# Latent queries prepared in the retention stage, and unsplit fp32 products at the start of two stages

## The reference, cut to what matters

```
cq, ckv, kr, rq, rk, rv, rg, ga, gb = split(x @ w_in)
q     = (rms_norm(cq, q_norm_g) @ w_q_up)           # latent queries, 256 wide
o_ret = retention_chunked(rope(rq), rope(rk) * RET_DK ** -0.5, rv)   # 4 heads
o_mla = attention(q, rms_norm(ckv), rope(kr), ...)  # 8 heads
mixed = (sigmoid(ga) * (o_mla @ w_mla_o) + sigmoid(gb) * (ret @ w_ret_o)) @ w_out
h     = layer_norm(ALPHA * x + mixed)
out   = layer_norm(ALPHA * h + shared_expert(h) + routed_experts(h))
```

## Time and profile before

| what | value |
|---|---|
| median of three runs | 1898.04 us |
| the three runs | 1894.51, 1898.04, 1899.26 us |
| the profiled execution | 1883.99 us |
| its span, first to last instruction | 1882.2 us |
| mean granted TensorE clock | 0.979 of 2.4 GHz |
| start of attention, mixing, trunk in the span | 497.2, 729.0, 827.9 us |
| MB moved, packets | 411.62, 133020 |

### The profile page before, as it was taken

The page is one execution under the profiler, slowest core; times in us unless marked ns, Lnnn a source line. Parts: engine busy times, 40 slices in busy tenths (PEclk is TensorE's granted clock), DMA queues, the critical chain, the costliest instruction groups (busy, mean ns, idle before and its releaser), DMA issues. The chain is left out here.

```text
span 1882.2 us, 24592 instructions
## 1 busy us (share of the span) xinstructions
PE 1780.7 (95%) x8660; PEld 1222.0 (65%) x8660; DVE 690.2 (37%) x1482; ACT 422.0 (22%) x862; POOL 351.7 (19%) x288
## 2 busy tenths in 40 slices
PE   7999999999899998999999999999999999999990
PEld 7999999999655556988865444444444444544440
DVE  3112444443256555645775222222222222222225
ACT  3111221322345453211100011111111111111114
POOL 0000330430100000001156111222222222222213
PEclk9999999999899999999999999999999999999995
DMA  6331633442312217441252689999999999999966
GB/s 213 100 103 52 189 108 107 154 129 72 127 31 71 61 42 269 169 155 59 82 227 47 259 313 379 380 386 381 388 369 365 370 368 370 369 368 367 349 183 215
DMA packets 133020, 411.62 MB, mean 219 GB/s; under 512 B 17620, under 2 KB 79092, under 8 KB 115332
## 3 DMA queue, kind: packets, MB, share of 16 engines
q1 hardware_dynamic: 108418, 319.77, 45.5%
q0 software_dynamic: 21504, 73.87, 15.0%
q10 hardware_dynamic: 3026, 17.04, 2.2%
HBM read 339.11 MB, written 73.96 MB: 219 GB/s over the span
## 5 line engine op out<-in xcount | busy, mean ns | idle before, releaser
L2397 PE MATMUL e_G<-wb,pages 128*128 128x512 f32 x1072 | 471.1, 592 | 1.8 <-DMA wb<-in_w_exp_gu 1.5
L2397 PEld LDWEIGHTS e_G<-wb,pages 128*128 128x128 f32 x1072 | 203.5, 190 | 258.3 <-issue 258.3
L2388 PE MATMUL e_Y<-mixT,e_aT 128*128 128x512 f32 x544 | 246.0, 595 | 2.4 <-ACT e_aT L2259 2.4
L2230 POOL DMA_INDIRECT d_base<-e_y_sb,e_s_idx x68 | 107.7, 1584 | 584.9 <-DMA d_base<-e_y_sb,e_s_idx 531.0
L2388 PEld LDWEIGHTS e_Y<-mixT,e_aT 128*128 128x128 f32 x544 | 98.0, 190 | 101.2 <-issue 100.6
L1293 PE MATMUL gate_ps<-x_hi,gw_hi 128*128 128x352 f32 x464 | 151.7, 327 | 1.4 <-DVE r_srg L1096 1.4
L181 PE MATMUL ps<-w_hi,x_hi 128*128 128x244 f32 x512 | 142.9, 279 | 9.8 <-DVE x_lo L235 8.7
L1293 PE MATMUL gate_ps<-x_hi,gw_lo 128*128 128x352 f32 x464 | 149.4, 322 | 0.0
L1293 PE MATMUL gate_ps<-x_lo,gw_hi 128*128 128x352 f32 x464 | 149.0, 321 | 0.0
L181 PE MATMUL ps<-w_hi,x_lo 128*128 128x244 f32 x512 | 142.1, 278 | 0.0
L181 PE MATMUL ps<-w_lo,x_hi 128*128 128x244 f32 x512 | 141.7, 277 | 0.0
(11 more groups left out here) (410 smaller groups left out, 2708.0 us busy)
## 6 DMA issues: line engine op xcount, KB each, us to landing
wb<-in_w_exp_gu SPq DMA_DIRECT2D x64, 2048.0 KB, 13.0
mixT<-in_w_exp_dn SPq DMA_DIRECT2D x68, 1024.0 KB, 7.3
gw_sb<-in_w_gate SPq DMA_DIRECT2D x20, 512.0 KB, 6.8
d_proj<-o_sb SPq DMA_DIRECT2D x8, 1098.0 KB, 6.2
d_gateT<-r_g_out ACTq DMA_DIRECT2D x16, 528.0 KB, 2.7
pages<-in_cache_both SPq DMA_DIRECT2D x64, 128.0 KB, 2.0
wb<-in_w_exp_gu ACTq DMA_DIRECT2D x4, 2048.0 KB, 15.2
w_sb<-in_w_in SPq DMA_DIRECT2D x7, 976.0 KB, 11.1
```

Of the source, the lines that this page charges most:

```text
L2230: g.indirect_dma_start(base, bass.IndirectOffsetOnAxis(ap=s_idx[s][:, 0:1], axis=0), y_sb[:, c, :], None, compute_op=ALU.add).then_inc(y_o ...
L2388: mm = t_.matmul(Y[q][:], aT[:, c, k, :], w_d[:, s, k, q * 512:(q + 1) * 512], start=k == 0, stop=k == 1)
L2397: mm = t_.matmul(G[c], xT[:, c, k, :], w_gu[s][:, :, k, :], start=k == 0, stop=k == KD - 1)
```

## The change

Latent queries: their load moves from the start of attention to SP's list in retention's last head, into the memory of `raw_q` and `raw_k` (now one tile) once both rotations are done. VectorE squares them, sums them and takes the mean after `nbias` of the last head; GpSimd takes the power; VectorE scales them after `gained`. ScalarE's squares, VectorE's and GpSimd's steps and SP's wait leave attention. The tile `cq` in attention is placed at the same address.

Mixing: A of j = 0 is made from the unsplit fp32 tiles (12 products of 352 columns, c outermost, 24 matmul records), so its weights are not split, and oT is split after rT and the first half of j = 1's weights. VectorE's `unit` is cut in two, and the first two A multiplications of j = 0 are put between the last oT splits. SP's load of j = 2's weights goes ahead of the two 2 MB loads.

Trunk: the first four of eight k steps of `out(0, 1)` are made from unsplit fp32 tiles ahead of everything else (4 products of 512 columns, 8 records); the right half of w_out is split from k = 4 on; the order becomes out_raw, out(0, 0), out(0, 1) without those steps, out(1, 0), out(1, 1).

```diff
@@ attention: tiles and loads @@
-        stat = sb("stat", [P, 2, NT])
-        mhalf = sb("mhalf", [P, NT])
...
-        cq = turned_flat[:, 0:NT * QL].rearrange("p (t c) -> p t c", t=NT)
+        cq = nc.alloc_sbuf_tensor_at("t_cq", [P, NT, QL], F32, offset=cq_at)
         rt = turned_flat[:, NT * (QL + KVL):NT * (QL + KVL) + 4 * TC].rearrange("p (a s c) -> p a s c", a=2, s=2)
-        sq_q = turned_flat[:, 5120:5120 + QL]
...
             sp.dma_start(wuv[:], a["w_uv"]).then_inc(w_kv_in, 16)
-            sp.dma_start(cq, pv[:, :, 0:QL]).then_inc(cq_in, 16)
             sp.dma_start(qg[:], a["q_norm_gT"]).then_inc(const_in, 16)
-            sp.wait_ge(cq_in, 16)
             sp.dma_start(w_q.rearrange("p k b n -> p (k b n)"), a["w_q_ext"]).then_inc(w_in_s, 16)
...
-            g.memset(mhalf[:], -0.5).then_inc(pl, 1)
             g.memset(bd[:], 0.0).then_inc(bd_clear, 1)
-            pool.wait_ge(pl, 1)
-            pool.wait_ge(dv, 1)
-            g.tensor_tensor(stat[:, 1, :], stat[:, 0, :], mhalf[:], ALU.pow).then_inc(pl, 1)
-
-            pool.wait_ge(pl, 2)
+            pool.wait_ge(bd_clear, 1)
             pool.wait_ge(krT_ok, 2)
...
-                if u == 4:
-                    dve.wait_ge(sq_ok, NT)
-                    v.tensor_scalar(stat[:, 0, :], stat[:, 0, :], 1.0 / QL, RMS_EPS, ALU.mult, ALU.add).then_inc(dv, 1)
-            dve.wait_ge(pl, 2)
-            v.tensor_tensor(cq, cq, stat[:, 1, :].unsqueeze(2).broadcast_to([P, NT, QL]), ALU.mult).then_inc(cq_ok, 1)
...
-            act.wait_ge(cq_in, 16)
-            for t in range(NT):
-                act.wait_ge(sq_ok, t)
-                s_.activation(sq_q, cq[:, t, :], ACT.Square, accum_out=stat[:, 0, t:t + 1]).then_inc(sq_ok, 1)
...
-            pe.wait_ge(cq_ok, 1)
@@ retention @@
+        cq_at = nc.sbuf_base
+        raw_qk = sb("raw_qk", [P, 2, NT, P])
+        raw_q, raw_k = raw_qk[:, 0], raw_qk[:, 1]
+        cq = raw_qk[:].rearrange("p a t c -> p (a t c)").rearrange("p (t c) -> p t c", t=NT)
...
-        tq = sb("tq", [P, 2, NT, 64])
-        tk = sb("tk", [P, 2, NT, 64])
+        tqk = sb("tqk", [P, 2, 2, NT, 64])
+        tq, tk = tqk[:, 0], tqk[:, 1]
+        cq_squares = tqk[:].rearrange("p a b t c -> p (a b t c)").rearrange("p (t c) -> p t c", t=NT)
+        cq_s = sb("cq_s", [P, 2, NT])
...
+                    if i == 3 and h == HR - 1:
+                        sp.wait_ge(q_rot, 6 * HR)
+                        sp.wait_ge(k_rot, 6 * HR)
+                        sp.dma_start(cq, pv[:, :, 0:QL]).then_inc(cq_in, 16)
...
+            pool.wait_ge(cq_var, 1)
+            g.tensor_tensor(cq_s[:, 1, :], cq_s[:, 0, :], mhalf[:], ALU.pow).then_inc(cq_rstd, 1)
...
+            dve.wait_ge(cq_in, 16)
+            dve.wait_ge(q_rot, 6 * HR)
+            dve.wait_ge(k_rot, 6 * HR)
+            v.tensor_tensor(cq_squares, cq, cq, ALU.mult).then_inc(cq_dv, 1)
+            dve.wait_ge(cq_dv, 1)
+            v.tensor_reduce(cq_s[:, 0, :], cq_squares, AX.X, ALU.add).then_inc(cq_dv, 1)
+            dve.wait_ge(cq_dv, 2)
+            v.tensor_scalar(cq_s[:, 0, :], cq_s[:, 0, :], 1.0 / QL, RMS_EPS, ALU.mult, ALU.add).then_inc(cq_var, 1)
             gained(HR - 1)
+            dve.wait_ge(cq_rstd, 1)
+            v.tensor_tensor(cq, cq, cq_s[:, 1, :].unsqueeze(2).broadcast_to([P, NT, QL]), ALU.mult).then_inc(cq_dv, 1)
+            dve.wait_ge(cq_dv, 3)
@@ mixing @@
+            def weights(j):
+                sp.wait_ge(w_hi_ok, 2 * j - 3)
+                sp.wait_ge(w_lo_ok, 2 * j - 3)
+                sp.dma_start(w_raw[:, j % 2], a["w_mix"][j]).then_inc(w_in_s[j % 2], 16)
+            sp.wait_ge(a_done, 3)
+            weights(2)
             sp.wait_ge(o_hi_ok, 4)
             sp.wait_ge(o_lo_ok, 4)
             sp.dma_start(wo_raw, a["w_out"].rearrange("(k p) n -> p k n", p=P)[:, :, 0:512]).then_inc(wo_in, 16)
@@ -1427,9 +1435,8 @@
             sp.wait_ge(r_lo_ok, 4)
             sp.dma_start(pages[:, 0:KD * 512].rearrange("p (k n) -> p k n", k=KD), a["w_out"].rearrange("(k p) n -> p k n", p=P)[:, :, 512:D]).then_inc(wo1_in, 16)
             for j in range(2, KD):
-                sp.wait_ge(w_hi_ok, 2 * j - 2)
-                sp.wait_ge(w_lo_ok, 2 * j - 2)
-                sp.dma_start(w_raw[:, j % 2], a["w_mix"][j]).then_inc(w_in_s[j % 2], 16)
+                if j > 2:
+                    weights(j)
 
...
-            weights(0, 0)
-            for k in range(4):
-                s_.copy(oT_hi[:, k], oT[:, k]).then_inc(o_hi_ok, 1)
             weights(0, 1)
             act.wait_ge(r_in, 64)
             for k in range(4):
                 s_.copy(rT_hi[:, k], r_raw[:, k]).then_inc(r_hi_ok, 1)
-            for q in range(2):
-                weights(1, q)
+            weights(1, 0)
+            for k in range(4):
+                s_.copy(oT_hi[:, k], oT[:, k]).then_inc(o_hi_ok, 1)
+            weights(1, 1)
             for q in range(2):
                 weights(2, q)
...
-                dve.wait_ge(w_hi_ok, 2 * j + q + 1)
+                dve.wait_ge(w_hi_ok, 2 * j + q)
...
-            weights(0, 0)
-            for k in range(4):
+            def o_part(k):
                 dve.wait_ge(o_hi_ok, k + 1)
                 v.tensor_tensor(oT_lo[:, k], oT[:, k], oT_hi[:, k].bitcast(F32), ALU.subtract).then_inc(o_lo_ok, 1)
             weights(0, 1)
             for k in range(4):
                 r_part(k)
-            for q in range(2):
-                weights(1, q)
+            weights(1, 0)
+            for k in range(3):
+                o_part(k)
+            first_product(0, 0)
+            o_part(3)
+            first_product(0, 1)
+            weights(1, 1)
             for j in range(KD):
                 for c in range(3):
                     if j == 3:
                         wo_residue(3 * c, min(3 * c + 3, KD))
                     if j == 4 and c == 0:
                         dve.wait_ge(wo_lo_ok, KD)
-                    unit(j, c)
+                    if j or c == 2:
+                        first_product(j, c)
+                    second_product(j, c)
                     if c == 0 and j and j + 1 < KD:
                         for q in range(2):
                             weights(j + 1, q)
@@ -1536,7 +1552,9 @@
...
-                    pe.wait_ge(w_lo_ok, 2 * j + 1)
+                    pe.wait_ge(w_lo_ok, 2 * j)
+                if u == 3:
+                    pe.wait_ge(o_lo_ok, 4)
...
-                    pe.wait_ge(w_lo_ok, 2 * j + 2)
+                    pe.wait_ge(w_lo_ok, 2 * j + 1)
                 if u >= 3:
                     pe.wait_ge(tb_ok, u - 2)
                 part(B[u % 3], 4, rT_hi, rT_lo, j, c).then_inc(b_done, 1)
-            def first_part(out, w0, hi, lo, hi_ok, lo_ok, done):
-
-                pe.wait_ge(w_lo_ok, w0 // 4 + 1)
+            pe.wait_ge(w_in_s[0], 16)
+            for c in range(3):
                 for k in range(4):
-                    pe.wait_ge(hi_ok, k + 1)
-                    pe.wait_ge(lo_ok, k + 1)
-                    for c in range(3):
-                        at = slice(c * TC, (c + 1) * TC)
-                        for s, (w, x) in enumerate(((w_hi, hi), (w_hi, lo), (w_lo, hi))):
-                            mm = t_.matmul(out[c][:, 0:TC], w[:, 0, w0 + k, :], x[:, k, at], start=k == 0 and s == 0, stop=k == 3 and s == 2)
-                        if k == 3:
-                            mm.then_inc(done, 1)
-            first_part(A, 0, oT_hi, oT_lo, o_hi_ok, o_lo_ok, a_done)
-            first_part(B, 4, rT_hi, rT_lo, r_hi_ok, r_lo_ok, b_done)
+                    mm = t_.matmul(A[c][:, 0:TC], w_raw[:, 0, k, :], oT[:, k, c * TC:(c + 1) * TC], start=k == 0, stop=k == 3)
+                mm.then_inc(a_done, 1)
+            pe.wait_ge(w_lo_ok, 1)
+            for k in range(4):
+                pe.wait_ge(r_lo_ok, k + 1)
+                for c in range(3):
+                    at = slice(c * TC, (c + 1) * TC)
+                    for s, (w, x) in enumerate(((w_hi, rT_hi), (w_hi, rT_lo), (w_lo, rT_hi))):
+                        mm = t_.matmul(B[c][:, 0:TC], w[:, 0, 4 + k, :], x[:, k, at], start=k == 0 and s == 0, stop=k == 3 and s == 2)
+                    if k == 3:
+                        mm.then_inc(b_done, 1)
             for j in range(1, KD):
                 for c in range(3):
@@ trunk @@
             sp.wait_ge(wo1_hi_ok, KD)
             sp.wait_ge(wo1_lo_ok, KD)
+            sp.wait_ge(y_raw, 1)
             sp.dma_start(w_gu[:, :, 0:256], a["w_sh_gate"].rearrange("(k p) n -> p k n", p=P)).then_inc(w_in_s, 16)
...
-            for k in range(KD):
+            for n in range(KD):
+                k = (n + 4) % KD
                 s_.copy(wo1_hi[:, k], w_gu[:, k]).then_inc(wo1_hi_ok, 1)
...
-                dve.wait_ge(wo1_hi_ok, k + 1)
+            for n in range(KD):
+                k = (n + 4) % KD
+                dve.wait_ge(wo1_hi_ok, n + 1)
                 v.tensor_tensor(wo1_lo[:, k], w_gu[:, k], wo1_hi[:, k].bitcast(F32), ALU.subtract).then_inc(wo1_lo_ok, 1)
```

(38 more changed lines are left out.)

6 lines of the change are left out of this document (2 added, 4 removed).

## The result

| | before | changed |
|---|---|---|
| median of 5 runs | 1898.04 us | 1887.49 us |
| lowest and highest | 1894.51, 1903.57 us | 1883.25, 1891.36 us |
| profiled execution | 1883.99 us, span 1882.2 | 1884.30 us, span 1882.5 |

The ratio is 0.9937, with a 95% interval of 0.9915 to 0.9958: 10.55 us less by the medians, 8 to 16 by the interval. The two profiled executions, though, are equally long. Each stage on which the change works is shorter in the new profile, and what was won is gone again at trunk's end. Both have to be explained.

A forecast was written before the change was run, and what follows sets the result against it. TensorE, busy 95% of the span, was taken as the bound. Attention 6.6, mixing 3.7 - 1.4 and trunk 4.1 - 1.4 sum to 11.6 us, so 1898.04 becomes 1886.4 us, range 1881 to 1894.

The forecast's parts named there:

- I take 6.6, because the idle time that preceded the fall is gone: Attention's start: 3.55 us idle before the value product and 3.03 us of its lower clock level both won.
- the zero: Retention's last head: the latent queries' load and arithmetic, moved there, are covered by TensorE's last gate unit and cost 0.
- clock term: Mixing's start: a short clock fall after about 2 us idle takes 1.4 us off the 3.7 us gain.
- the 4.1 of the text: Trunk's start: end at 850.4 against 854.58, 4.1 us won at the full clock.
- the 1.9 us row: Wait at trunk's end, followed by a 0.57 clock over 3.2 us; taken as model for a 1.4 us loss.
- The 1.4 us at both starts: Mixing and trunk: a short clock fall after about 2 us idle, costing 1.4 us each.
- carrying the difference over: Whole kernel: the 11.6 us gain, figured on the 1883.99 us profiled execution, subtracted from the 1898.04 us median.
- The fifth: Mixing: w_out loads issued 6 us later on SP's queue delay j = 3's weights, making the kernel slower; chance 0.03.
- The third: Mixing and trunk: plain parts run at 1.2 GHz to their end, leaving 3.7 us won, 1894.3; chance 0.07.
- the fourth: Attention: the value product still waits, for w_uv or another copy, leaving 5.0 us won, 1893.0; chance 0.04.
- The first: Mixing and trunk: no clock fall at one or both starts, 13.0 or 14.4 us won, down to 1883.6; chance 0.25.
- The second: A small term fails: values stay at 1.2 GHz (3.0 less), or j = 1 stalls on oT residues (1891.4); chance 0.16.

The follow-up runs named there:

- cover run: Changed kernel with squares and sum of the latent queries made four times over in the retention's last head; 1883.77 us in one execution.
- load alone: Changed kernel with only the latent queries' load left in retention; squares, mean, power and scaling back in attention; ratio 0.9935.
- mixing kernel: Kernel before with only mixing's new start, attention and trunk as before; ratio 0.9979.
- paced kernel: Changed kernel with a memset of 128 x 128 on GpSimd after each of the 54 indirect transfers of the token list; ratio 0.9873, 1876.5 us.

## Why the prediction was right, and where it was not

Forecast 1886.4 us, measured 1887.49: 11.6 us against 10.55. The terms, by the stretches of all profiled executions:

| | before, mean | changed, mean | gain | forecast |
|---|---|---|---|---|
| attention, to the first query product | 26.4 (4) | 23.0 (8) | 3.4 | 6.6 |
| mixing, to j = 1 | 16.8 (4) | 14.6 (9) | 2.2 | 2.3 |
| trunk, to the first transposition | 37.2 (4) | 34.0 (10) | 3.2 | 2.7 |

The numbers in brackets are executions. Attention is counted from its first product and its mean leaves out the cover run and the load alone; mixing and trunk are counted from 1.9 and 2.0 us after TensorE's last record before them, and mixing's mean leaves out the cover run. The gains sum to 8.8 us, inside the intervals of both comparisons; the other 1.7 us of the 10.55 are put down to nothing here.

**Attention: right in kind, 3.2 us too large.** The wait and its cause were as told, and in the first pair of profiles the term measured 28.33 - 21.85 = 6.5. The step that failed is "I take 6.6, because the idle time that preceded the fall is gone". It took one execution's load time for the kernel's, and it counted the lower level of the value product as won although TensorE comes out of the 4.5 us change of stage at that level anyway: when the clock rises late, the key products pay (8.96 us instead of 7.22). Five of the eight executions had this, three did not; with the old attention one of four did (8.25 us, the mixing kernel's), and that one had no slow value product. That the wait itself was the load's, and not the squares', the text did not ask; the load alone brings the whole gain.

**Retention: right.** All prices and the zero. The cover is 6.7 us and not 7.8, since the way into attention takes 1.26 us of it.

**Mixing: right, with its clock term.** The fall came in 9 of 10 executions, the one without it had 12.89 us to j = 1: 1.6 us, where I had 1.4. j = 1 did not wait; the residues of oT and the second half of the weights were done at 732.3, 1.3 us ahead of it. Bringing forward the weights of j = 2 was counted as safer and free; undone, it costs 5.9 us in one execution, so it belongs to the gain.

**Trunk: the sum was right, the clock was not as told.** Without a fall the gain is 37.48 - 33.48 = 4.0 us, the 4.1 of the text (the mixing kernel's 36.50, shorter by 1 us than the other three with the old trunk, left out). The fall that I took from the 1.9 us row came in 3 executions of 10, at 1.7 us. The 1.4 us at both starts were one guess; mixing confirmed it, trunk mostly did not. The Trainium skill (TensorE: Matmul & The Clock Gate, "HAM oscillation — how this bites in real kernels") warns only of longer gaps. By that section neither start would fall; trunk agrees in 7 executions of 10, mixing in 1.

**The profiled execution's 14 us: found.** I wrote that nothing in the profile tells where the other executions are longer. All but that one have 7 to 15 us of stalls at trunk's end, and carrying the difference over was right, because both kernels have them. The stretch in which they lie, from trunk's first transposition to the first expert's product, took 204.0 us on average in the four executions with the old start of trunk and 203.6 in the six with the new one and the list as it was. Without it the profiled executions are comparable: 1883.99 - 190.4 = 1693.6 and 1896.12 - 206.8 = 1689.3 before, 1884.30 - 206.5 = 1677.8 and 1883.74 - 202.8 = 1680.9 after, 8 to 16 us apart.

**The rivals.** The fifth (SP's queue) was looked for in the right place: a load that comes late there does cost TensorE, but the order in the change avoids it. The third (plain parts slow to their end) and the fourth (the value product still waits) came in none of the executions. The first came at trunk, in 7 executions of 10. The second is nearest to what happened in attention, 1.7 us of it in 5 executions of 8.

## What to carry to other kernels

Where a wait is put down to work that itself waited for a load, move the load first; the arithmetic may stay. Read a term from several executions when a transfer's landing is in it, and add up stages rather than totals when a few us are asked for. And look for stalls without a releaser beside long series of small indirect transfers: pacing them won more here than the whole change.

## What was not expected of the hardware

**Small indirect transfers at a close pace stall other engines.** The list is written by 54 indirect transfers from GpSimd, each of 128 rows. Issued every 1.26 us, they make TensorE and VectorE wait in steps of about 0.7 us (0.67, 1.36, 2.05) near the end of each series: 7 to 15 us in nine of ten executions that left pace and groups as they were, 29.2 with all in one block. No fixed number of transfers sets this off: in the first profile the series of 18 has it from 21.8 us after its first transfer on, the block of 54 only from 39 us on. At 1.36 us they remain (12.5), at 1.46 us 1.1 are left, at 1.94 none. The paced kernel's six runs are faster too, so the stalls are not the one profiled execution's. In the block of 54, from 1005 to 1035 us, the profile has no packet of any other queue, and none that loads instructions; the kernel before, from 1005 to 1030 us, has 578 of loads and stores and one of instructions. Whether that is cause or consequence, what the engines wait for, and whether recording the profile has a part in it, was not tried. Nor is it known why one execution of the kernel before had none.

**A wait of 2.9 us in full flow cost 5.9 us in its one execution**, half of it afterwards, at half the clock. And equal idle times of 1.9 to 2.0 us were followed by the lower level in 9 of 10 cases at one place and in 3 of 10 at another; the runs do not show what makes the difference.
